# Seven products in place of eight for the last two value blocks of a 2048-wide input projection

## Chip, cores and metric

One NeuronCore of a Trainium2 chip runs one program that computes two transformer blocks over 256 tokens of width 2048. The metric is the device time in microseconds of that program, the median of its runs. The times are in us throughout.

## The reference, cut to what matters

The first block starts with gated linear attention. Its input projection gives queries and keys (1024 columns each), values and output gates (2048 each) and 16 columns of a low-rank gate.

```python
def _gla_mixer(h, w_in, w_gate_up, b_gate, o_norm, w_out):
    proj = h @ w_in
    q, k, v, r, g_low = jnp.split(proj, [...], axis=-1)
    log_a = jax.nn.log_sigmoid(g_low @ w_gate_up + b_gate) / 16
    # chunks of 64 tokens, 4 heads: state = decay * state + k^T v, o = q state
    ...
    return (rmsnorm(o) * o_norm * jax.nn.silu(r)) @ w_out

h = h + _gla_mixer(_rmsnorm(h, gla_norm), ...)
h = h + _sq_relu_mlp(_rmsnorm(h, mlp_norm), ...)
# second block: a hybrid of three attentions, cross-attention to a memory, a gated FFN
```

Here `h @ w_in` is 256 x 2048 times 2048 x 6160, in float32. What the change touches are 1024 of its columns: value columns 1024 to 2047.

## The kernel before

**Numbers.** All large products run in three parts. A float32 weight w is split into a high part (`w_hi`, rounded to the matmul's 32-bit format) and a low part (`w_lo`, the rest), the activations likewise, and TensorE adds high x high, high x low and low x high. So each piece of weights costs ScalarE one rounding copy (line 1226, `split` of ScalarE) and VectorE one subtraction (line 1912, `split` of VectorE), both 128x2048.

**Chunks.** The weights of the whole program are one stream of 1 MB pieces, 128 partitions x 4 x 512: four blocks of 128 input rows (a quarter `q` of the 2048) times 512 output columns (a block `b`). TensorE's `chunk` (lines 632 to 648) multiplies one piece with both halves of the tokens (m = 0, 1): 4 x 2 x 3 = 24 matmuls of 128x128 by 128x512, into the accumulator `acc[:, b % 2]`. Four chunks in turn finish a block. The input projection is items 0 to 47: blocks 0, 1 queries, 2, 3 keys, 4 to 7 values, 8 to 11 output gates.

**The ring.** `SLOTS = 4` pieces are resident in `w_raw` (the low part is written in place, `w_lo`) and in `w_hi`. SyncE loads piece n when item n - 4 is used (line 533). All engines walk the same list of steps, each in its own program order: at step c ScalarE and VectorE split item c + 3 (`AHEAD = 3`), ScalarE when item c - 1 is used, VectorE when the high part is there. TensorE takes item c when its low part is ready. So an item's low part is made while the three before it are multiplied.

**Side work by steps.** The order is written out by hand. After each finished block ScalarE evacuates the accumulator with the row scale (line 1243): to `nat` for queries and keys, to `v` for values. VectorE turns `nat` to the transposed layout in 32x32 tiles (`block_turned`, line 2065): at steps 8, 10 the queries, at steps 20, 24 the keys, each as 8 + 8 transposes with the split of that step between. At step 26 it multiplies the keys with their decay (line 2096), at step 27 the queries of head 0 (`scaled_q`, line 2004). TensorE computes the scores of head hd at step 33 + 4 hd and the products with the values at step 34 + 4 hd (`gla_scores`, `gla_values`). The decays are computed on the way; `la_diff` reaches 2 when the last of them is formed (line 2092).

**Pairs of blocks in seven products.** Elsewhere the kernel already computes two neighbouring blocks with fewer multiplications: for the upper half of the input rows (q = 0, 1) and two column blocks the 2 x 2 x 2 half-size products are replaced by seven (Strassen's scheme in Winograd's form), each of 12 matmuls (`product`); the lower half (q = 2, 3) stays as four chunks. This costs additions: sums of token halves (`s_raw`, with high and low parts `s_hi`, `s_lo`, lines 2118 to 2127) and sums of weight pieces (`T1` to `T4`, lines 2140 to 2150), which enter the list of items as additional ones without a load of their own. In the first MLP pair (`up_pair`, items 8 to 18 of a group of 38, from about 424 us) and in the six like it in the MLP this stands already, and in two pairs of the last FFN: nine in all (`PAIRS`). In the MLP the four sums of rows are lines 2121 to 2124, the second and third sums of weights lines 2143 and 2145.

Of the kernel before, what the change touches and what calls it, by code (L numbers as in the profile page):

```python
# [2 lines left out]
P = 128  # L3
# [14 lines left out]
def build(nc, x, x_turned, mem, mem_turned, stream, cols, rows, wglow, wab, wgu, shapes, masks, out):  # L18
# [23 lines left out]
    PAIRS = GROUPS + 5  # L42
# [5 lines left out]
    with ExitStack() as ctx:  # L48
# [99 lines left out]
        for t in ("f1", "f2", "f3", "f4", "f22"):  # L148
            sum_raw[t] = sb(f"raw_{t}", [P, CH], F32, a_sum[t])
            sum_lo[t] = sb(f"lo_{t}", [P, CH], F32R, a_sum[t])  # L150
# [131 lines left out]
        down_out = sem("down_out")  # L282
        OUT = {name: k for k, name in enumerate(("p1", "p6", "p7", "up2", "up3", "s"))}
# [150 lines left out]
        C_GLA, C_OUT, C_MLP, C_2 = 0, 48, 64, 64 + sum(LENGTH)  # L434
# [12 lines left out]

        def sum_of(i):

            if i >= C_FFN:  # L450
# [11 lines left out]

        def up_chunk(g, q, b):
            return C_MLP + 32 * g + 4 * b + q

        def down_chunk(g, q, b):
            return C_MLP + 32 * g + 16 + 4 * b + q
# [4 lines left out]
        def source(i):  # L472

            if i < C_MLP:
                return i
# [10 lines left out]
            return C_MLP + 32 * g + (k if k < 8 else k - 3)  # L486
# [10 lines left out]
        def summed(i):  # L497

            n = pair_of(i)
            return 4 * n + SUMS[2 if n >= 7 else n % 2].index(sum_of(i)) + 1  # L500
# [5 lines left out]
        def _(sp):  # L506
# [115 lines left out]
        def _(pe):  # L622
# [114 lines left out]
            def gla_values(hd):  # L737
                g = tps.name[("o", hd)]
                open_group(g)
                tps.wait(pe, tps.name[("s", hd)])  # L740
# [12 lines left out]

            pe.wait_ge(junk_set, 1)
            for _ in range(13):
                pe.matmul(acc[:, 1, 0, :], junk[:, 0:P], junk[:], start=True, stop=True)
            for c in range(48):
                b, q = divmod(c, 4)
                chunk(C_GLA + c, X, 4 * q, accs.name[("gla", b)], q == 0, q == 3)
# [18 lines left out]

            def product(c, xh, xl, dst, start=False, stop=False):

                pe.wait_ge(lo_ready, ready(c))
                wh = w_hi[:, c % SLOTS].rearrange("p (k n) -> p k n", n=N)
                wl = low_part(c).rearrange("p (k n) -> p k n", n=N)
                for k in range(4):
                    pe.matmul(dst, xh[:, k], wh[:, k], start=start and k == 0, stop=False, skip_group_check=not start)  # L785
                    pe.matmul(dst, xh[:, k], wl[:, k], start=False, stop=False, skip_group_check=not start)  # L786
                    mm = pe.matmul(dst, xl[:, k], wh[:, k], start=False, stop=stop and k == 3, skip_group_check=not start)  # L787
                mm.then_inc(used, 1)

            def up_pair(g):  # L790
# [17 lines left out]
                if g == 0:  # L808
                    pe.wait_ge(s_formed, 2)
# [46 lines left out]
            for g in range(GROUPS):  # L856
# [11 lines left out]
                if g < 3:  # L868
                    pe.wait_ge(pair_out, pair_step(g, "p7"))
                    down_pair(C_MLP + GROUP * g, accs.name["down", g, 2], accs.name["down", g, 3], (u_hi, u_lo), 2 * g + 4, 5 * g)  # L870
# [315 lines left out]
            for g in range(2):  # L1186
                for c in range(48):
# [3 lines left out]
                    if c == 40:  # L1191
                        down_pair(F_PART[g] + 13, accs.name["fdown", g, 2], accs.name["fdown", g, 3], (uf_hi, uf_lo), 10 + 2 * g, 15 + 5 * g, g == 1)
                        break
# [12 lines left out]
        def _(act):  # L1206
# [8 lines left out]
            def split(c):  # L1215

                if c < NITEM:
                    if sum_of(c) in ("b22", "d22", "f22"):
# [76 lines left out]
            def gla_side(c):  # L1295
# [8 lines left out]
                for hd in range(4):  # L1304
# [13 lines left out]
                    if c == 35 + 4 * hd:  # L1318

                        act.wait_ge(used, c + 1)  # L1320
# [25 lines left out]
            for c in range(64):  # L1346
# [6 lines left out]
                for n in {7: (0, 1), 11: (2,), 15: (3,), 19: (4,), 23: (5,), 27: (6,), 31: (7,)}.get(c, ()):  # L1353
# [49 lines left out]
                if c:  # L1403
                    split(c + AHEAD)
# [41 lines left out]
            for part in range(4):  # L1446
                for c in range(LENGTH[part]):
# [26 lines left out]
                    if part == 0 and c == 6:  # L1474
                        act.wait_ge(s_formed, 1)
                        act.activation(s_hi[:].rearrange("p s k t -> p (s k t)"), s_raw[:].rearrange("p s k t -> p (s k t)"), ACT.Copy).then_inc(pair_out, 1)
                    if part < 3 and c == 23:
                        act.wait_ge(s_formed, 2 * part + 3)
# [356 lines left out]
            for part in range(2):  # L1835
                for c in range(51):
# [22 lines left out]
                    if c == 37:  # L1859
                        act.wait_ge(s_formed, 9 + 2 * part)  # L1860
# [38 lines left out]
        def _(dve):  # L1899
# [169 lines left out]
            for c in range(64):  # L2069
# [23 lines left out]
                if c == 26:  # L2093
# [5 lines left out]
                if c == 27:  # L2099
                    dve.wait_ge(kd_exp, 2)  # L2100
                    scaled_q(0)
                gla_side(c)
                if c - 48 in (6, 7, 11, 15):
                    n = (6, 7, 11, 15).index(c - 48)
                    add_to_h(("glaout", n), n, last=c)
# [5 lines left out]
                if c and c not in (8, 10, 20, 24):  # L2111
                    split(c + AHEAD)
# [871 lines left out]
```

## Time and profile before

| | us |
|---|---|
| median of 3 runs | 2467.79 (2467.27 to 2468.34) |
| the profiled execution | 2466.79 |
| its span, first to last instruction | 2464.6 |
| busy: TensorE / VectorE / ScalarE / GpSimd | 2453.2 / 1710.7 / 1624.5 / 33.4 |
| mean granted TensorE clock | 0.999 of full speed |

How to read the rows below. PE is TensorE's matmuls, PEld its loads of weights, DVE VectorE, ACT ScalarE, POOL GpSimd, SP SyncE, which issues most transfers. A row names the line of the kernel, the operation, the tile written and those read. In a timeline row the first number is the start, the second the time from there to the end of the last of the merged instructions; the bracket holds idle time ahead of it and what ended it. A matmul's duration (0.39) is longer than the distance to the next, since matmuls are pipelined; the distance is the cost.

### The profile page before, as it was taken

The numbers are of one execution on the slowest core, as the hardware profiler recorded it, in microseconds if no ns is written. First come the engines' busy times: TensorE is split into PE (matmuls) and PEld (weight loads), VectorE is DVE, ScalarE is ACT, GpSimd is POOL, SyncE is SP. The second block draws the span as 40 slices with busy tenths as digits, with TensorE's granted clock in tenths as the row PEclk, the third lists the DMA queues.
The fourth block names the chain that finished last, engine by engine and source line by source line (L and its number), as shares of the span: only waits on it lengthen the run. The fifth ranks groups of instructions, "written<-read, shape, count | busy, mean of one in ns | idle before, by whom it ended". The sixth has DMA issues, their size and how long they took to land.

```text
span 2464.6 us, 29831 instructions
## 1 busy us (share of the span) xinstructions
PE 2453.2 (100%) x12343; PEld 2026.5 (82%) x12343; DVE 1710.7 (69%) x1412; ACT 1624.5 (66%) x2127; POOL 33.4 (1%) x41
## 2 busy tenths in 40 slices
PE   9999999999999999999999999999999999999998
PEld 7887788888888888888888888888888888888887
DVE  5775658787778868577765685545666667776678
ACT  6645778856748658776465684535587688748874
POOL 0000000000000000000000000000000000000000
PEclk9999999999999999999999999999999999999999
DMA  8554456545554555545443455555654555645563
GB/s 290 188 191 168 174 188 239 188 182 210 206 204 174 219 208 188 188 172 193 159 148 140 155 185 188 194 199 188 263 198 172 188 190 198 227 171 188 193 233 120
DMA packets 69366, 472.36 MB, mean 192 GB/s; under 512 B 7912, under 2 KB 8352, under 8 KB 13424
## 3 DMA queue, kind: packets, MB, share of 16 engines
q1 hardware_dynamic: 67040, 460.62, 51.5%
q0 software_dynamic: 1312, 7.73, 0.8%
q8 instruction: 97, 1.59, 0.3%
q10 hardware_dynamic: 880, 2.11, 0.2%
q14 instruction: 37, 0.30, 0.0%
HBM read 468.33 MB, written 2.11 MB: 191 GB/s over the span
## 4 chain that ended last, share of the span: by engine, by line
PE 96%; DVE 2%; ACT 1%; issue 1%; DMA 0%; SPq 0%; POOLq 0%; POOL 0%; DVEq 0%; ACTq 0%
PE acc L643 29%; PE acc L644 28%; PE acc L645 28%; PE tp L787 1%; PE tp L785 1%; PE tp L786 1%; PE acc L785 1%; PE acc L787 1%; PE acc L786 1%; DVE w_lo L1912 1%; PE tp L1011 1%; PE tp L944 0%; PE tp L663 0%; DMA w_raw<-in_stream 0%; DVE lo_f L1912 0%
## 5 line engine op out<-in xcount | busy, mean ns | idle before, releaser
L1912 DVE TENSOR_TENSOR w_lo<-w_raw,w_hi 128x2048 fp32r<-128x2048 f32 x412 | 941.2, 2287 | 574.4 <-ACT w_hi L1226 572.6
L1226 ACT ACTIVATE w_hi<-w_raw 128x2048 fp32r<-128x2048 f32 x412 | 788.0, 1915 | 363.4 <-DMA w_raw<-in_stream 303.6
L643 PE MATMUL acc<-w_hi,x_hi 128*128 128x512 f32 (+1 forms) x2112 | 825.3, 391 | 0.7 <-issue 0.3
L644 PE MATMUL acc<-w_lo,x_hi 128*128 128x512 f32 (+1 forms) x2112 | 818.6, 388 | 0.0
L645 PE MATMUL acc<-w_hi,x_lo 128*128 128x512 f32 (+1 forms) x2112 | 818.6, 388 | 0.0
L643 PEld LDWEIGHTS acc<-w_hi,x_hi 128*128 128x128 f32 x2112 | 396.7, 188 | 85.5 <-issue 2.5
L645 PEld LDWEIGHTS acc<-w_hi,x_lo 128*128 128x128 f32 x2112 | 396.6, 188 | 82.0
L644 PEld LDWEIGHTS acc<-w_lo,x_hi 128*128 128x128 f32 x2112 | 396.9, 188 | 80.0 <-issue 1.0
L643 PE MATMUL acc<-w_hi,a_hi 128*128 128x512 f32 x960 | 374.2, 390 | 0.1
L645 PE MATMUL acc<-w_hi,a_lo 128*128 128x512 f32 x960 | 373.5, 389 | 0.0
L644 PE MATMUL acc<-w_lo,a_hi 128*128 128x512 f32 x960 | 373.5, 389 | 0.0
L643 PEld LDWEIGHTS acc<-w_hi,a_hi 128*128 128x128 f32 x960 | 180.2, 188 | 38.2 <-DVE a_lo L2693 0.5
L645 PEld LDWEIGHTS acc<-w_hi,a_lo 128*128 128x128 f32 x960 | 180.2, 188 | 37.5
L644 PEld LDWEIGHTS acc<-w_lo,a_hi 128*128 128x128 f32 x960 | 180.2, 188 | 37.0
L1419 ACT ACTIVATE sq<-turned 32x256 f32<-32x256 f32 x256 | 106.3, 415 | 6.8 <-DVE turned L2247 3.4
L1816 ACT ACTIVATE fm<-fturned 32x256 f32<-32x256 f32 x256 | 106.2, 415 | 4.4 <-DVE fturned L2799 1.4
L1243 ACT ACTIVATE nat<-acc,rstd 128x512 f32<-128x512 f32 (+1 forms) x80 | 50.0, 677 | 73.9 <-PE acc L645 72.5
L1243 ACT ACTIVATE nat<-acc,rhalf 128x512 f32<-128x512 f32 x36 | 22.8, 685 | 66.1 <-PE acc L645 66.1
L1988 DVE TENSOR_TENSOR h<-acc,h 128x1024 f32<-128x1024 f32 x34 | 41.4, 1219 | 18.6 <-PE acc L645 18.6
L1265 ACT ACTIVATE sq<-turned 32x256 f32<-32x256 f32 x112 | 46.5, 415 | 10.2 <-DVE turned L1955 8.9
L643 PE MATMUL acc<-w_hi,m_hi 128*128 128x512 f32 x128 | 49.8, 389 | 0.0
L644 PE MATMUL acc<-w_lo,m_hi 128*128 128x512 f32 x128 | 49.8, 389 | 0.0
(523 smaller groups left out, 2139.4 us busy)
## 6 DMA issues: line engine op xcount, KB each, us to landing
w_raw<-in_stream SPq DMA_DIRECT2D x412, 1024.0 KB, 4.8
w_raw<-in_stream SPq DMA_DIRECT2D x16, 256.0 KB, 7.8
raw_T<-in_stream SPq DMA_DIRECT2D x4, 1024.0 KB, 7.5
raw_b<-in_stream SPq DMA_DIRECT2D x4, 1024.0 KB, 9.2
raw_f<-in_stream SPq DMA_DIRECT2D x4, 1024.0 KB, 8.0
raw_t<-in_stream SPq DMA_DIRECT2D x3, 1024.0 KB, 7.0
raw_d<-in_stream SPq DMA_DIRECT2D x3, 1024.0 KB, 10.2
h<-in_x SPq DMA_DIRECT2D x4, 512.0 KB, 14.7
```

Source lines behind the costliest of these rows:

```text
L643: pe.matmul(dst, xh, wh[:, k], start=first and k == 0, stop=False)
L644: pe.matmul(dst, xh, wl[:, k], start=False, stop=False)
L645: mm = pe.matmul(dst, xl, wh[:, k], start=False, stop=last and k == n_k - 1)
L785: pe.matmul(dst, xh[:, k], wh[:, k], start=start and k == 0, stop=False, skip_group_check=not start)
L786: pe.matmul(dst, xh[:, k], wl[:, k], start=False, stop=False, skip_group_check=not start)
L787: mm = pe.matmul(dst, xl[:, k], wh[:, k], start=False, stop=stop and k == 3, skip_group_check=not start)
L1226: act.activation(w_hi[:, c % SLOTS], raw(c), ACT.Copy).then_inc(hi_ready, 1)
L1243: ins = act.activation(dst[:, m], src[:, m], func, scale=scales[:, j, m:m + 1])
L1265: ins = act.activation(dst[32 * to:32 * to + 32, :, :, q], src[32 * q:32 * q + 32, :, :, to], ACT.Copy, scale=scale)
L1419: ins = act.activation(dst[32 * to:32 * to + 32, :, :, q], src[32 * q:32 * q + 32, :, :, to], ACT.Square)
L1816: ins = act.activation(dst[32 * to:32 * to + 32, :, :, q], src[32 * q:32 * q + 32, :, :, to], ACT.Copy)
L1912: dve.tensor_tensor(low_part(c), raw(c), w_hi[:, c % SLOTS].bitcast(F32), ALU.subtract).then_inc(lo_ready, 1)
```

## The change

Value blocks 2 and 3 of the projection (accumulator blocks 6 and 7, items 24 to 31) are computed in the scheme of seven products. The list of items grows by three there: items 24 to 34 are the pair (`V_PAIR = 16`, its k runs from 8 to 18), the output gates move from items 32 to 47 to items 35 to 50, everything behind by three. On each engine:

- SyncE issues, behind the load of item 22, two more loads for pieces (q 0, b 3) and (q 1, b 3) of the value columns into `g3` and `g22`, after `la_diff` is 2. Their pieces are no longer loaded by the ring, so the bytes stay equal.
- VectorE forms sums of x at step 3 and of its rows at step 19, their low part at step 22, the sums of weights g1, g3, g2, g4 at steps 21, 22, 23, 26, and adds the partial results to `v` at steps 33, 34, 35. It splits three more items. The scaling of the keys moves from step 26 to 28, that of head 0's queries from 27 to 31. The turning of the keys at steps 20 and 24 is as before.
- ScalarE rounds the sums of rows at step 21, copies the shared partial result out of PSUM at steps 26, 30 and 32 (four copies), scales the values at steps 33 and 36 where it evacuated them at steps 27 and 31, and splits three more items.
- TensorE runs `v_pair` for items 24 to 34.

```diff
-        for n in range(8):
+        for n in range(6):
             accs.add(("gla", n), "act")
-        for n in range(8, 12):
+        for n in range(6, 12):
             accs.add(("gla", n), "dve")
...
+        V_SUM_AT = {10: "g22", 12: "g1", 13: "g2", 15: "g3", 16: "g4"}
...
+                if c == V_PAIR + 6:
+                    sp.wait_ge(la_diff, 2)
+                    sp.dma_start(sum_raw["g3"][:], stream[v_chunk(0, 3)]).then_inc(v_b_in, 16)
+                    sp.dma_start(sum_raw["g22"][:], stream[v_chunk(1, 3)]).then_inc(v_b_in, 16)
...
+            def v_pair():
...
+                tps.wait(pe, tps.name["z1"])
+                product(c0 + 8, *of_x(0, 0), chain, start=True, stop=True)
+                chunk(c0 + 9, X, 8, left, True, False)
+                pe.wait_ge(s_formed, 2)
+                accs.wait(pe, right - 2)
+                product(c0 + 10, *of_s(3), acc[:, right % 2, 0], start=True)
+                chunk(c0 + 11, X, 12, left, False, True)
+                product(c0 + 12, *of_s(0), both, start=True, stop=True)
+                pe.wait_ge(v_taken, 2)
+                product(c0 + 13, *of_s(1), chain, stop=True)
+                product(c0 + 14, *of_x(1, 0), acc[:, left % 2, 0], stop=True)
+                pe.wait_ge(v_taken, 3)
+                product(c0 + 15, *of_s(2), chain, stop=True)
+                product(c0 + 16, *of_x(1, 1), acc[:, left % 2, 1], stop=True)
+                chunk(c0 + 17, X, 8, right, False, False, rows_=(0,), done=False)
+                chunk(c0 + 17, X, 8, right, True, False, rows_=(1,))
+                chunk(c0 + 18, X, 12, right, False, True)
...
+            def v_sums(i):
...
+                if i == 19:
+                    dve.tensor_tensor(s_raw[:, 2], rows_[0][0], rows_[1][0], ALU.subtract)
+                    link(dve.tensor_tensor(s_raw[:, 0], rows_[1][0], rows_[1][1], ALU.subtract))
+                    link(dve.tensor_tensor(s_raw[:, 1], s_raw[:, 0], rows_[0][0], ALU.subtract))
+                    dve.tensor_tensor(s_raw[:, 3], s_raw[:, 1], rows_[0][1], ALU.add).then_inc(s_formed, 1)
+                if i == 22:
+                    dve.wait_ge(v_taken, 1)
+                    dve.tensor_tensor(s_lo[:], s_raw[:], s_hi[:].bitcast(F32), ALU.subtract).then_inc(s_formed, 1)
+            def v_pair(k):
...
+                if k == 5:
+                    b11 = weights_in(8)
+                    dve.wait_ge(v_b_in, 32)
+                    dve.tensor_tensor(sum_raw["g1"][:], b11, sum_raw["g3"][:], ALU.add).then_inc(v_sum_ready, 1)
+                if k == 6:
...
+                    dve.tensor_tensor(sum_raw["g3"][:], sum_raw["g3"][:], sum_raw["g22"][:], ALU.add).then_inc(v_sum_ready, 1)
+                if k == 7:
+                    dve.tensor_tensor(sum_raw["g2"][:], sum_raw["g1"][:], sum_raw["g22"][:], ALU.add).then_inc(v_sum_ready, 1)
+                if k == 10:
+                    b21 = weights_in(14)
+                    dve.wait_ge(used, V_PAIR + 11)
...
+                    dve.tensor_tensor(sum_raw["g4"][:], sum_raw["g2"][:], b21, ALU.add).then_inc(v_sum_ready, 1)
...
+            for i in range(67):
+                c = i if i < 32 else i - 3 if i >= 35 else -1
+                v_pair(i - V_PAIR)
...
-                if c == 26:
+                if c == 28:
                     dve.wait_ge(kd_exp, 1)
                     dve.wait_ge(q_turned, 4)
                     link(dve.tensor_tensor(kT[:], kT[:], kd[:], ALU.mult))
...
-                if c == 27:
+                if c == 31:
                     dve.wait_ge(kd_exp, 2)
+                    dve.wait_ge(used, V_PAIR + 14)
                     scaled_q(0)
...
-                if c and c not in (8, 10, 20, 24):
-                    split(c + AHEAD)
+                if i and i not in (8, 10, 20, 24):
+                    split(i + AHEAD)
+                v_sums(i)
```

## Rows read from the trace of the kernel before

**Rows 1.** The page, its parts 1 (busy us, share) and 4 (chain).

```profile
PE 2453.2 (100%) x12343; PEld 2026.5 (82%) x12343; DVE 1710.7 (69%) x1412; ACT 1624.5 (66%) x2127; POOL 33.4 (1%) x41
...
PE 96%; DVE 2%; ACT 1%; issue 1%; DMA 0%; SPq 0%; POOLq 0%; POOL 0%; DVEq 0%; ACTq 0%
```

**Rows 2.** TensorE's waits over the span: total, times, longest; first and last of seven.

```profile
PE acc L756 <- DVE junk L2042: 1.2, 1, 1.2
...
PE tp L892 <- DVE cqT L2333: 0.2, 1, 0.2
```

**Rows 3.** TensorE's timeline, 100 us on: first and 57th matmul without a gap.

```profile
99.76 0.39 PE L644 MATMUL acc<-w_lo,x_hi 128*128 128x512 f32 x1
...
112.45 0.39 PE L643 MATMUL acc<-w_hi,x_hi 128*128 128x512 f32 x1
```

**Rows 4.** ScalarE's timeline, 56 to 146 us: evacuations (L1243) and a high part.

```profile
56.01 1.27 ACT L1243 ACTIVATE nat<-acc,rstd 128x512 f32<-128x512 f32 x2 [1.12 <-PE acc L645]
...
122.85 1.26 ACT L1243 ACTIVATE v<-acc,rstd 128x512 f32<-128x512 f32 x2 [4.07 <-PE acc L645]
124.01 1.91 ACT L1226 ACTIVATE w_hi<-w_raw 128x2048 fp32r<-128x2048 f32 x1
...
144.61 1.26 ACT L1243 ACTIVATE v<-acc,rstd 128x512 f32<-128x512 f32 x2 [4.22 <-PE acc L645]
```

**Rows 5.** Busy time of the engines in two stretches: length; PE, PEld, DVE, ACT, POOL.

```profile
125.95:168.65 42.70, 42.70 (x190) 35.35 (x189) 35.63 (x46) 16.86 (x12) 0.00 (x0) 1.00 0.54 190
398.00:455.00 57.00, 57.00 (x252) 46.95 (x251) 51.55 (x33) 45.15 (x55) 0.71 (x1) 1.00 0.50 182
```

**Rows 6.** VectorE's timeline, 43 to 167 us: low parts (L1912), key turning, key scaling.

```profile
43.72 2.29 DVE L1912 TENSOR_TENSOR w_lo<-w_raw,w_hi 128x2048 fp32r<-128x2048 f32 x1 [0.22 <-ACT w_hi L1226]
...
116.52 0.17 DVE L2092 TENSOR_TENSOR edec<-edec,cum 128x8 f32<-128x8 f32 x1
...
125.95 2.29 DVE L1912 TENSOR_TENSOR w_lo<-w_raw,w_hi 128x2048 fp32r<-128x2048 f32 x1 [4.85 <-ACT w_hi L1226]
128.16 3.57 DVE L2065 STREAM_TRANSPOSE kT<-nat 32x256 f32<-32x256 f32 x8
131.75 2.29 DVE L1912 TENSOR_TENSOR w_lo<-w_raw,w_hi 128x2048 fp32r<-128x2048 f32 x1
134.07 3.60 DVE L2065 STREAM_TRANSPOSE kT<-nat 32x256 f32<-32x256 f32 x8
137.69 2.29 DVE L1912 TENSOR_TENSOR w_lo<-w_raw,w_hi 128x2048 fp32r<-128x2048 f32 x1
...
161.66 2.28 DVE L2096 TENSOR_TENSOR kT<-kT,kd 128x2048 f32<-128x2048 f32 x1
...
164.37 2.29 DVE L1912 TENSOR_TENSOR w_lo<-w_raw,w_hi 128x2048 fp32r<-128x2048 f32 x1
```

**Rows 7.** VectorE's timeline in the first MLP pair: the operations that the change adds.

```profile
401.67 2.35 DVE L2118 TENSOR_TENSOR x_sum<-x_hi,x_lo 128x1024 f32<-128x1024 f32 x2
...
407.40 0.68 DVE L2121 TENSOR_TENSOR s_raw<-x_sum 128x512 f32<-128x512 f32 x1
...
409.44 0.69 DVE L2124 TENSOR_TENSOR s_raw<-s_raw,x_sum 128x512 f32<-128x512 f32 x1
...
421.44 2.28 DVE L2145 TENSOR_TENSOR raw_T<-raw_T,raw_b 128x2048 f32<-128x2048 f32 x1
423.65 2.28 DVE L1912 TENSOR_TENSOR w_lo<-w_raw,w_hi 128x2048 fp32r<-128x2048 f32 x1
```

**Rows 8.** Transfers issued from 325 to 465 us: count, size, median us to landing.

```profile
w_raw<-in_stream SPq DMA_DIRECT2D x25, 1024.0 KB, 4.9
raw_T<-in_stream SPq DMA_DIRECT2D x1, 1024.0 KB, 6.9
raw_b<-in_stream SPq DMA_DIRECT2D x1, 1024.0 KB, 8.9
```

**Rows 9.** TensorE's timeline at the start: the 13 matmuls on a zeroed tile.

```profile
1.19 5.73 PE L756 MATMUL acc<-junk 128*128 128x512 bf16 x13 [1.19 <-DVE junk L2042]
```

More of the change, by code:

```diff
@@ L41, in build @@
     LENGTH = [38, 38, 38, 35]
-    PAIRS = GROUPS + 5
+    PAIRS = GROUPS + 6
     NITEM = stream.shape[0] + 3 * PAIRS
@@ L432, in build @@
             add_quarter(6, n)
-        C_GLA, C_OUT, C_MLP, C_2 = 0, 48, 64, 64 + sum(LENGTH)
+        C_GLA, C_OUT, C_MLP, C_2 = 0, 51, 67, 67 + sum(LENGTH)
+        V_PAIR = 16
         C_BR, C_WO, C_X, C_XO, C_FFN = C_2 + 50, C_2 + 114, C_2 + 130, C_2 + 142, C_2 + 146
@@ L739, in gla_values @@
                 open_group(g)
+                if hd == 0:
+                    accs.wait(pe, accs.name["gla", 7])
                 tps.wait(pe, tps.name[("s", hd)])
@@ L751, in gla_side, with product, of_x, of_s @@
                         gla_values(hd)
+            def product(c, xh, xl, dst, start=False, stop=False):
+                pe.wait_ge(lo_ready, ready(c))
+                wh = w_hi[:, c % SLOTS].rearrange("p (k n) -> p k n", n=N)
+                wl = low_part(c).rearrange("p (k n) -> p k n", n=N)
+                for k in range(4):
+                    pe.matmul(dst, xh[:, k], wh[:, k], start=start and k == 0, stop=False, skip_group_check=not start)
+                    pe.matmul(dst, xh[:, k], wl[:, k], start=False, stop=False, skip_group_check=not start)
+                    mm = pe.matmul(dst, xl[:, k], wh[:, k], start=False, stop=stop and k == 3, skip_group_check=not start)
+                mm.then_inc(used, 1)
+            def v_pair():
+                c0, left, right = V_PAIR, accs.name["gla", 6], accs.name["gla", 7]
+                chain, both = tpf(0)[:, 0:N], tpf(0)[:, N:2 * N]
+                def of_x(q, m):
+                    return [t[:, 4 * q:4 * q + 4, m * P:(m + 1) * P] for t in X]
+                def of_s(n):
+                    return s_hi[:, n], s_lo[:, n]
+                tps.wait(pe, tps.name["z1"])
[15 more added lines that the diff above has]
+                chunk(c0 + 18, X, 12, right, False, True)
             pe.wait_ge(junk_set, 1)
@@ L757, in _ @@
             for c in range(48):
+                if c == 24:
+                    v_pair()
+                if 24 <= c < 32:
+                    continue
                 b, q = divmod(c, 4)
-                chunk(C_GLA + c, X, 4 * q, accs.name[("gla", b)], q == 0, q == 3)
+                chunk(C_GLA + (c if c < 24 else c + 3), X, 4 * q, accs.name[("gla", b)], q == 0, q == 3)
                 if c == 3:
@@ L777, in _ @@
                 gla_side(48 + c)
[L779 to L788, printed above, removed]
             def up_pair(g):
@@ L1345, in _ @@
             act.activation(wg[:, :, 0:16], wg_raw[:], ACT.Copy).then_inc(wg_h, 1)
-            for c in range(64):
+            def v_pair(k):
+                left, right = [slice(n * N, (n + 1) * N) for n in (2, 3)]
+                chain = tpf(0)[:, 0:N]
+                if k == 5:
+                    act.wait_ge(s_formed, 1)
+                    act.activation(s_hi[:].rearrange("p s k t -> p (s k t)"), s_raw[:].rearrange("p s k t -> p (s k t)"), ACT.Copy).then_inc(v_taken, 1)
+                if k == 10:
+                    act.wait_ge(used, V_PAIR + 9)
+                    act.activation(v[:, 0, left], chain, ACT.Copy).then_inc(v_taken, 1)
+                if k == 14:
+                    act.wait_ge(used, V_PAIR + 14)
+                    act.activation(v[:, 0, right], chain, ACT.Copy, scale=-1.0).then_inc(v_taken, 1)
+                if k == 16:
+                    act.wait_ge(used, V_PAIR + 16)
+                    act.activation(v[:, 1, left], chain, ACT.Copy)
+                    act.activation(v[:, 1, right], chain, ACT.Copy, scale=-1.0).then_inc(v_taken, 1)
+                if k == 17:
+                    accs.wait(act, accs.name["gla", 6])
+                    row_scaled(0, v[:, :, left], v[:, :, left])
+                if k == 20:
+                    accs.wait(act, accs.name["gla", 7])
+                    row_scaled(0, v[:, :, right], v[:, :, right])
+            for i in range(67):
+                c = i if i < 32 else i - 3 if i >= 35 else -1
+                v_pair(i - V_PAIR)
                 if c == 4:
@@ L2067, in block_turned @@
                     ins.then_inc(q_turned, 1)
-            for c in range(64):
+            def v_sums(i):
+                rows_ = [[x_sum[:, q, :, m * P:(m + 1) * P] for q in range(2)] for m in range(M)]
+                if i == 3:
+                    for q in range(2):
+                        ins = dve.tensor_tensor(x_sum[:, q], x_hi[:, 4 * q:4 * q + 4].bitcast(F32), x_lo[:, 4 * q:4 * q + 4].bitcast(F32), ALU.add)
+                    link(ins)
+                if i == 19:
[6 more added lines that the diff above has]
+                    dve.tensor_tensor(s_lo[:], s_raw[:], s_hi[:].bitcast(F32), ALU.subtract).then_inc(s_formed, 1)
@@ L2070, in _ @@
+            for i in range(67):
+                c = i if i < 32 else i - 3 if i >= 35 else -1
+                v_pair(i - V_PAIR)
                 if c == 6:
@@ L2104, in _ @@
                     n = (6, 7, 11, 15).index(c - 48)
-                    add_to_h(("glaout", n), n, last=c)
+                    add_to_h(("glaout", n), n, last=i)
                     norm_turned(1, n, ("glaout", n))
```

68 lines of the change are left out of this document (53 added, 15 removed).

## The prediction

> **What bounds the kernel now.** I read the page first, then TensorE's waits, then the two engines that feed it. TensorE is busy for the whole span and nearly the whole chain that ended last is TensorE's [rows 1]. Its longest wait is 1.2 us at the very start; the view names seven kinds, from this one down to 0.2 us, and they come to 3.3 us in all [rows 2]. So the time is the number of matmuls times their cadence, as long as VectorE delivers every low part in time. The cadence of the 128x512 matmuls is (112.45 - 99.76) / 56 = 0.2266 us [rows 3]. A chunk is 24 of them, 5.44 us; ScalarE's evacuations of value blocks 0 and 1 (from chunks 19 and 23) come 144.61 - 122.85 = 21.76 us apart, four chunks [rows 4], the same number. A half chunk (one `product`, 12 matmuls) is 2.72 us.
>
> The second view to read is VectorE in the stretch that changes. From 125.95 to 168.65 us it is busy 35.6 of 42.7 us [rows 5]; its idle time lies ahead of low parts and ends with ScalarE's high part [rows 6]. That is not a bound today, but it is little room.
>
> **What is removed.** The old loop spends 8 chunks, 192 matmuls, on value blocks 2 and 3. The new `v_pair` has seven products of 12 and four chunks of 24: 84 + 96 = 180. Twelve matmuls go: 12 x 0.2266 = 2.72 us of pure TensorE time. That is the whole possible gain, 0.11% of 2467.79. About 0.2% (4.9 us) is what a measurement of this kernel can tell from no change. With nothing late, the result would be 2465.1.
>
> **What is added.** In place of 8 items (24 to 31) there are 11 (24 to 34). Each item is one upper part on ScalarE (1.91 us) and one low part on VectorE (2.29 us, 2.20 to 2.21 from start to start when they follow on) [rows 4, 6, 7]. So three more of each. VectorE also gets: the two sums of x at step 3 (2.35 us [rows 7]); four formings of sums of rows at step 19 (four 128x512 additions, 407.40 to 410.13, 2.73 us [rows 7]); their low part at step 22; four sums of weights (g1, g3, g2, g4) of one 128x2048 addition each at steps 21 to 26; three 128x1024 additions at steps 33 to 35. What VectorE already does there stays: the turning of the keys in four runs of eight transposes at steps 20 and 24, 3.59 and 3.62 us a run, and the scaling of the keys [rows 6]. The scaling of keys goes from step 26 to 28 and that of queries from 27 to 31. Both still stand ahead of a low part in VectorE's order. In the diff the turning of the keys itself isn't touched.
>
> **The sum, on VectorE.** VectorE works in order, so I add what lies between two fixed points. The first is the start of the low part of item 22 at 125.95: it waits for the upper part that ScalarE makes from 124.01 on, right after its evacuation at 122.85, which itself waits for chunk 19 [rows 4, 6]. Nothing of the change moves that, and work cannot slide ahead of it. The second is the low part of item 31. Between them, in program order (g1, g3, s_lo, g2, g4 are the additions of 128x2048):
> - low parts 22 to 31: 10 x 2.21 = 22.1, and 0.1 more for each of the two that a run of transposes follows (131.75 to 134.07 is 2.32 [rows 6]): 22.3
> - the four formings: 2.7
> - the four runs of transposes: 2 x 3.59 + 2 x 3.62 = 14.4
> - g1, g3, g2, g4 and s_lo: 5 x 2.20 = 11.0 (the same operations took this in the first MLP pair [rows 7])
> - scaling of the keys and two memsets, 161.66 to 164.37 [rows 6]: 2.7
>
> Together 53.1 us: low part 31 is finished at 125.95 + 53.1 + 0.1 = 179.15. When does TensorE want it? Chunk 23's result is there at 144.61 [rows 4]. Items 24 to 30 hold nine half chunks (1, 2, 1, 2, 1, 1, 1): 9 x 2.72 = 24.5, so item 31 is due to begin at 169.1 on that scale. A first matmul starts some 0.2 us ahead of the preceding result and has its load of weights, 0.19 us, before it, so the low part is wanted about 0.4 earlier, at 168.7. It comes 179.15 - 168.7 = 10.45 us late. Walking item by item with the same durations spreads it: item 24 waits 0.7, 25 1.7, 26 1.2, 27 3.1 (the whole first run of key transposes stands ahead of it), 28 0.5, 29 1.7, 31 1.7, together 10.6. The same walk over the old order, begun at 51 us, puts low part 29 at 164.34 where the trace has it at 164.37 [rows 6], which is why I trust it.
>
> From item 32 on the low parts catch up: item 32 has 0.5 us of slack, 33 has 1.0, 34 has 3.2, 35 has 5.3, since items 33 and 34 are full chunks and no more sums stand between. Net: 10.5 - 2.7 = **+7.8 us**.
>
> **What costs nothing, and its cover.** ScalarE: the rounding of the sums (1.9), three more upper parts and four copies out of PSUM. It is busy 16.9 of 42.7 us in the stretch [rows 5] and its upper parts are ready before VectorE comes to each. TensorE's waits for the copies: the copy after item 29 is needed after item 30, 2.7 us later, and takes half of an evacuation, 0.64 [rows 4]. SyncE: the two added transfers wait for `la_diff` to be 2, which is true from 116.7 on [rows 6], while SyncE gets there at about 117.4; so this wait blocks nothing. The loads queued behind are the question. Load 23 issues at 122.9, when chunk 19 is done, and a load by itself takes 4.9 us to land [rows 8]. With 2 MB ahead of it in the queue, issued at about 118, it lands later; the same kind of pair took 6.9 and 8.9 us to land [rows 8], so the second is in at about 127 and load 23 some 2.5 us behind it, at about 130 instead of 127.8. Its upper part is then done at about 131.6, and VectorE reaches low part 23 only at 134.5. Cost 0; if the landing were 5 us later still, about 2 us, which I put into the upper end. The sums of x at step 3 lie ahead of low part 7. That one starts at 43.72 and takes 2.29 [rows 6]; item 7 is the last of its block, whose result is there at 56.01 [rows 4], so it is wanted at 56.01 - 5.44 - 0.4 = 50.2. The 4.2 us in hand cover the 2.35. The last additions and ScalarE's scaling of the values end near 203.5 in the walk, the values are first read after 212, and the block that follows needs its accumulator released at item 35, with 5 us to spare.
>
> Bounds of what no row shows: the sums' extra waits (0 each if they pass, 0.05 us for each of about 8 instructions as upper end), the pipeline delay at a stalled start (0.2 to 0.6 us instead of 0.4, once in the net), and VectorE's rate beside other work (the first MLP pair shows 2.2 for the same operations with ScalarE busy 45 of 57 us [rows 5, 7]). These make the net +7.3 to +8.6, and +10.5 with the late landing. Against that, if some of VectorE's operations overlap better than in any row, 3 us less: +4.5.
>
> **The rivals.** (A) Forecast: VectorE's backlog outweighs the matmuls saved: 2467.79 + 7.8 = **2475.6**; against the profiled execution (2466.79, span 2464.6) that is 2474.6 and a span of 2472.4. (B) The lead of three items absorbs it. Low part 22 is done at 128.2 and wanted at 133.3, so there are 5 us in hand before anything starts; in the first MLP pair VectorE is busy 51.6 of 57 us [rows 5] with sums and splits of the same sizes, and the list of TensorE's waits has none from there. It decides from the point where the sum above is 42.7 or less; it would take 10.4 us of VectorE's 53.1 to be gone or to fit before 125.95. Against it: in the first MLP pair no key turning (14.4) and scaling (2.7) stand between. Then 2465.1, the same within 0.2%. (C) The added transfers delay the ring so that ScalarE becomes late first: up to 2478. (D) TensorE's clock falls in the gaps. Today the granted clock is 1.00 in the stretches read [rows 5] and 0.999 over the span (table above), and the only slow matmuls are the 13 at the start, 5.73 / 13 = 0.44 us each, the level of 1.2 GHz [rows 9]. The longest new gap is 3.1 us, ahead of item 27. At half clock each half chunk in items 27 to 30 takes 5.4 instead of 2.7; while VectorE is the bound this is hidden in part (the five half chunks would take 13.6 more, of which the waits of 28, 29 and 31, 3.9 us, can absorb a share), so 5 to 10 us more: 2481 to 2486.
>
> The Trainium skill, page "TensorE: Matmul & The Clock Gate", Part 1, says that the array's clock is gated to half when TensorE has been idle long enough, which is the rule behind (D). This case's trace shows a granted clock of 1.00 throughout but has no gap of this kind after the start, so it neither confirms nor denies it; by the page the change could lose more than the waits, and without it the sum stands as above.
>
> **How the numbers follow.** (A) 0.78, (B) 0.10, (C) 0.05, (D) 0.05, and 0.02 for something in this first stage turning out faster than before. The range takes (A) with its bounds and (C): 2472.3 (net +4.5) to 2479.5; outside it stay (B), (D) and the rest. Slower by over 0.2% (above 2472.7): 0.86. Within 0.2%: 0.12. Faster by over 0.2%: 0.02.
>
> **What would show it.** In the profile after: TensorE's waits for another engine grow from about 3 us to about 14, nearly all on low parts (L1912's successor), between 144 and 180 us, at `product` and `chunk` alike, the largest ahead of item 27; VectorE without a gap from 126 to 179, ScalarE's upper parts ready before it; behind the pair the evacuations arrive about 7.8 us later than before (item 35 begins near 196 instead of 188) and this shift stays constant to the end. The forecast is wrong if TensorE shows no waits there (then B), if VectorE has gaps ended by ScalarE or a DMA (then C), or if the granted clock is under 1.00 after a gap (then D).

## The result and the profile after

| | before | after |
|---|---|---|
| median, us | 2467.79 (7 runs, 2467.21 to 2468.68) | 2475.06 (7 runs, 2474.01 to 2475.59) |
| ratio after / before | | 1.003, 95% interval 1.0021 to 1.0039 |
| profiled execution, its span | 2466.79, 2464.6 | 2475.24, 2473.4 |
| TensorE matmuls | 12343 | 12331 |
| busy TensorE / VectorE / ScalarE | 2453.2 / 1710.7 / 1624.5 | 2453.6 / 1736.3 / 1633.4 |

The changed kernel does its 12 matmuls less and is 7.3 us slower; 7.8 was forecast. The first view to open is again TensorE's waits, of the changed kernel between 100 and 200 us (who waited for whom; total, times, longest us):

```profile
PE acc L664 <- DVE w_lo L1999: 4.0, 2, 2.7
PE tp L783 <- DVE lo_g L1999: 2.0, 2, 1.4
PE acc L783 <- DVE lo_g L1999: 1.0, 1, 1.0
PE tp L783 <- DVE w_lo L1999: 0.4, 1, 0.4
```

The kernel before has no row in this stretch. All of these wait for a low part (L1999 is the subtraction that was L1912), at items 24 to 31, and for nothing else. L664 is in `chunk`, L783 in `product`. TensorE's timeline puts them in order, the bracket being the idle time:

```profile
145.84 0.47 PE L783 MATMUL tp<-w_hi,x_hi 128*128 128x512 f32 x1 [0.42 <-DVE w_lo L1999]
150.15 0.50 PE L664 MATMUL acc<-w_hi,x_hi 128*128 128x512 f32 x1 [1.31 <-DVE w_lo L1999]
156.85 0.47 PE L783 MATMUL acc<-w_hi,s_hi 128*128 128x512 f32 x1 [0.97 <-DVE lo_g L1999]
162.56 0.80 PE L664 MATMUL acc<-w_hi,x_hi 128*128 128x512 f32 x1 [2.70 <-DVE w_lo L1999]
173.00 0.47 PE L783 MATMUL tp<-w_hi,s_hi 128*128 128x512 f32 x1 [0.61 <-DVE lo_g L1999]
180.12 0.47 PE L783 MATMUL tp<-w_hi,s_hi 128*128 128x512 f32 x1 [1.39 <-DVE lo_g L1999]
```

These are items 24, 25, 26, 27, 29 and 31. The brackets sum to 7.4 us, less than what is lost: a matmul counts as busy for 0.39 us where the next could start after 0.23, which hides 0.16 of every wait; the second matmul behind a wait comes 0.31 to 0.34 us after the first instead of 0.23; and the clock, below, adds 1.5 us at item 27. The full loss is read from the ends. VectorE's timeline of the same kernel, with what the kernel before has as [rows 6]:

```profile
126.81 2.29 DVE L1999 TENSOR_TENSOR w_lo<-w_raw,w_hi 128x2048 fp32r<-128x2048 f32 x1 [4.85 <-ACT w_hi L1287]
129.02 0.68 DVE L2164 TENSOR_TENSOR s_raw<-x_sum 128x512 f32<-128x512 f32 x1
...
131.68 3.57 DVE L2152 STREAM_TRANSPOSE kT<-nat 32x256 f32<-32x256 f32 x8
135.26 2.29 DVE L1999 TENSOR_TENSOR w_lo<-w_raw,w_hi 128x2048 fp32r<-128x2048 f32 x1
137.58 3.59 DVE L2152 STREAM_TRANSPOSE kT<-nat 32x256 f32<-32x256 f32 x8
141.20 2.29 DVE L2183 TENSOR_TENSOR raw_g<-w_raw,raw_g 128x2048 f32<-128x2048 f32 x1
143.41 2.29 DVE L1999 TENSOR_TENSOR w_lo<-w_raw,w_hi 128x2048 fp32r<-128x2048 f32 x1
...
177.68 4.49 DVE L1999 TENSOR_TENSOR lo_g<-raw_g,w_hi 128x2048 fp32r<-128x2048 f32 x2
```

From 126.81 on no row has a bracket until 194: VectorE never waits there, and TensorE waits for nothing but its low parts. The low part of item 24 starts at 143.41, where the kernel before had it at 137.69. Low part 31 (the first of the two in the last row) ends at 177.68 + 2.29 = 179.97, and item 31's first matmul starts at 180.12, 0.15 later.

Everything in this execution is some 0.86 us later than in the profile before already at the first evacuations (ScalarE's second block at 56.87 for 56.01 [rows 4]), from two waits of 0.18 and 0.65 us for low parts of the very first pieces, at 6.3 and 10.2 us. That has nothing to do with the change: the first operation that the change adds starts at 44.30, and the experiments below on the kernel before have the same evacuation at 56.30 to 56.63. With 0.86 added, low part 31 was forecast for 180.0. ScalarE's evacuation behind chunk 23 is here at 145.46. Item 31 was due 24.5 us after the start of item 24's first matmul at 145.46 - 0.2, so at 169.8: it is 10.4 us late; 10.45 was forecast. The first addition to `h` starts at 330.80 before and at 339.43 after: 8.63 later, less 0.86 is 7.8.

The granted clock, as the stretches of TensorE show it (last three columns: clock, DMA share, GB/s):

```profile
155.00:160.00 5.00, 3.89 (x16) 2.56 (x15) 4.90 (x9) 1.96 (x2) 0.00 (x0) 1.00 0.58 205
160.00:165.00 5.00, 2.44 (x6) 1.96 (x7) 4.89 (x8) 1.86 (x1) 0.00 (x0) 0.71 0.02 8
165.00:170.00 5.00, 5.00 (x23) 4.10 (x22) 4.94 (x5) 0.24 (x1) 0.00 (x0) 0.95 0.00 0
```

After the wait of 2.70 us the clock had fallen: the first seven matmuls of item 27 (162.56 to 165.62) take 3.1 us instead of 1.6, 0.43 us apart, the lower level of 1.2 GHz; then 0.23 again. That is rival (D)'s mechanism, and by the prediction's own list ("if the granted clock is under 1.00 after a gap") the sign of (D). Its price is settled below.

### The profile page after: what moved, and what is told of

The parts are those of the page before. It is cut to its first block, busy times and chain, and to the rows that moved or that the text cites. A ratio compares the mean times of both kernels' runs of the same rounds, so it can differ in the third digit from the quotient of the medians.

```text
span 2473.4 us, 29846 instructions
## 1 busy us (share of the span) xinstructions
PE 2453.6 (99%) x12331; PEld 2024.5 (82%) x12331; DVE 1736.3 (70%) x1429; ACT 1633.4 (66%) x2135; POOL 33.5 (1%) x41
## 4 chain that ended last, share of the span: by engine, by line
PE 92%; DVE 4%; ACT 1%; issue 1%; DMA 1%; SPq 0%; POOLq 0%; POOL 0%; DVEq 0%; ACTq 0%
PE acc L664 27%; PE acc L665 27%; PE acc L666 27%; DVE w_lo L1999 1%; PE tp L783 1%; PE tp L785 1%; PE tp L784 1%; PE acc L783 1%; PE acc L785 1%; PE acc L784 1%; DMA w_raw<-in_stream 1%; ACT w_hi L1287 1%; DVE kT L2152 1%; PE tp L1068 1%; PE tp L1001 0%
## 5 line engine op out<-in xcount | busy, mean ns | idle before, releaser
L1999 DVE TENSOR_TENSOR w_lo<-w_raw,w_hi 128x2048 fp32r<-128x2048 f32 x410 | 936.5, 2287 | 554.3 <-ACT w_hi L1287 552.5
L664 PE MATMUL acc<-w_hi,x_hi 128*128 128x512 f32 (+1 forms) x2080 | 813.8, 391 | 5.7 <-DVE w_lo L1999 4.6
L666 PE MATMUL acc<-w_hi,x_lo 128*128 128x512 f32 (+1 forms) x2080 | 806.7, 388 | 0.0
L665 PE MATMUL acc<-w_lo,x_hi 128*128 128x512 f32 (+1 forms) x2080 | 806.6, 388 | 0.0
L664 PEld LDWEIGHTS acc<-w_hi,x_hi 128*128 128x128 f32 x2080 | 391.0, 188 | 91.1 <-DVE w_lo L1999 7.2
L666 PEld LDWEIGHTS acc<-w_hi,x_lo 128*128 128x128 f32 x2080 | 390.9, 188 | 80.5
L665 PEld LDWEIGHTS acc<-w_lo,x_hi 128*128 128x128 f32 x2080 | 391.1, 188 | 79.1 <-issue 1.0
L664 PE MATMUL acc<-w_hi,a_hi 128*128 128x512 f32 x960 | 374.1, 390 | 0.1
L664 PEld LDWEIGHTS acc<-w_hi,a_hi 128*128 128x128 f32 x960 | 180.2, 188 | 38.1 <-DVE a_lo L2835 0.5
L664 PE MATMUL acc<-w_hi,m_hi 128*128 128x512 f32 x128 | 49.8, 389 | 0.0
## 6 DMA issues: line engine op xcount, KB each, us to landing
raw_b<-in_stream SPq DMA_DIRECT2D x4, 1024.0 KB, 10.2
```

Of the source, the lines that this page charges most:

```text
L664: pe.matmul(dst, xh, wh[:, k], start=first and k == 0, stop=False)
L665: pe.matmul(dst, xh, wl[:, k], start=False, stop=False)
L666: mm = pe.matmul(dst, xl, wh[:, k], start=False, stop=last and k == n_k - 1)
L1999: dve.tensor_tensor(low_part(c), raw(c), w_hi[:, c % SLOTS].bitcast(F32), ALU.subtract).then_inc(lo_ready, 1)
```

## The experiments

Theory V is the forecast's: the work that VectorE does in order between low part 22 and low part 31 is longer than TensorE can wait. Rival T blames the added transfers and the ring, rival P the products themselves. Each kernel was timed beside the kernel before on the same chip; "against" is that one's median beside it. "By the trace" means the start of the first addition to `h` (330.80 us in the kernel before), less what the execution was already late at the first evacuations; by it the changed kernel is 7.8 us late.

### Key turning taken apart

```diff
-                if c in (8, 10, 20, 24):
+                if c in (8, 10):
...
+                for n, quadrants in {11: ((2, (0, 1)),), 12: ((2, (2,)),), 13: ((2, (3,)),), 17: ((3, (0,)),), 19: ((3, (1,)),), 20: ((3, (2,)),), 27: ((3, (3,)),)}.get(c, ()):
+                    accs.wait(dve, accs.name[("gla", n)])
+                    block_turned(n, quadrants)
...
-                if c == 28:
+                if c == 30:
                     dve.wait_ge(kd_exp, 1)
...
-                if i and i not in (8, 10, 20, 24):
+                if i and i not in (8, 10):
```

> The changed kernel with the turning of the keys taken apart: block 2's four quadrants at steps 11, 11, 12, 13, block 3's at steps 17, 19, 20, 27, and the scaling of the keys at step 30 instead of 28. Same operations, other places. Theory V (VectorE's in-order work from low part 22 to 31 sets TensorE's waits): five of the eight quadrants leave that stretch and fill idle time, 12.6 us of VectorE's 53 stay ahead no longer; my walk with the trace's durations gives no wait for a low part at all, so 2467.8 - 2.7 = 2465.1, and TensorE's waits in the stretch 0 to 0.5 us. Rival T (the added transfers and the ring make the items late): the waits stay near 8 to 10 us, 2473 to 2475. Rival P (the products cost by themselves, by waits for the partial results in PSUM or by restarts): 2469 or more.

Measured: 2464.89 us against 2467.22, ratio 0.9991 (0.9982 to 1.0). It was timed once more:

> The same kernel as the one with the key turning taken apart, once more beside the kernel before, for its interval: 2.7 us below it by V, 2464.6 to 2465.1.

2464.70 against 2467.34, ratio 0.9989 (0.998 to 0.9998). In the first one's profile TensorE has no wait between 100 and 215 us, with VectorE still almost always busy (its stretches; PE, PEld, DVE, ACT):

```profile
125.00:144.00 19.00, 19.00 (x86) 15.73 (x85) 18.72 (x18) 9.38 (x6) 0.00 (x0) 1.00 0.71 273
144.00:180.00 36.00, 36.00 (x161) 29.81 (x160) 35.07 (x25) 22.05 (x16) 0.00 (x0) 1.00 0.40 147
```

161 matmuls in the 36 us from 144 on. The changed kernel, in the same stretch:

```profile
144.00:180.00 36.00, 28.72 (x115) 21.76 (x113) 35.62 (x32) 18.40 (x13) 0.00 (x0) 0.95 0.35 120
```

Products, transfers, sums and TensorE's program are the same in both. So neither T nor P: with VectorE's work placed otherwise the 12 matmuls come back as 2.3 and 2.6 us, where 2.7 was worked out. This version is the fastest of the three, by 0.1% against the kernel before, which the second series of runs just tells from nothing (the first one's interval ends at 1.0).

VectorE's timeline shows where a piece went, here one quadrant of step 19 (x4, where a run was x8):

```profile
122.66 2.29 DVE L1999 TENSOR_TENSOR w_lo<-w_raw,w_hi 128x2048 fp32r<-128x2048 f32 x1 [2.12 <-ACT w_hi L1287]
124.99 1.78 DVE L2152 STREAM_TRANSPOSE kT<-nat 32x256 f32<-32x256 f32 x4
126.85 2.29 DVE L1999 TENSOR_TENSOR w_lo<-w_raw,w_hi 128x2048 fp32r<-128x2048 f32 x1
...
165.01 4.49 DVE L1999 TENSOR_TENSOR lo_g<-raw_g,w_hi 128x2048 fp32r<-128x2048 f32 x2
```

Before low part 22 there were 4.85 us of idle time; here a quadrant fills a part of them, and low part 22 still starts as soon as its high part is there. From its start to the end of low part 31 (165.01 + 2.29) it is 40.5 us, where the changed kernel needs 53.2: six of the eight quadrants (the expectation says five) and the scaling of the keys now stand outside. Low part 31 is done at 167.3. By the prediction's reckoning it is wanted at 169.6, ScalarE's evacuation behind chunk 23 being at 145.51 here, so TensorE doesn't wait.

The walk missed one thing. TensorE has one new wait, ahead of item 14, where two quadrants at step 11 now stand in front of the low part:

```profile
90.78 0.50 PE L664 MATMUL acc<-w_hi,x_hi 128*128 128x512 f32 x1 [0.30 <-DVE w_lo L1999]
```

By the trace this kernel is 2.1 us ahead of the kernel before in both series, so the placing itself costs about 0.6 of the 2.7.

### Only block 2's turning moved

```diff
-                if c in (8, 10, 20, 24):
+                if c in (8, 10, 24):
...
+                for n, quadrants in {11: ((2, (0, 1)),), 12: ((2, (2,)),), 13: ((2, (3,)),)}.get(c, ()):
...
```

> The changed kernel with only block 2's key turning moved (steps 11, 11, 12, 13 instead of 20), block 3's left at step 24. V: by the walk waits of 0.8, 0.5, 1.7 and 1.7 us ahead of items 27, 28, 29 and 31, none ahead of 24 to 26, together 4.6 instead of 10.5: 2467.8 + 4.6 - 2.7 = 2469.7. It is less than 7.2 us of transposes saved, since part of them would come to stand as idle time of VectorE. T or P: 2473 to 2475, with the waits ahead of 24 to 26 still there.

Measured: 2469.47 against 2467.22, ratio 1.0009 (1.0 to 1.0018). The waits, on TensorE's timeline, are those of the walk, one by one, once 0.2 to 0.3 us is added to each bracket (forecast 0.8, 0.5, 1.7, 1.7):

```profile
156.93 0.50 PE L664 MATMUL acc<-w_hi,x_hi 128*128 128x512 f32 x1 [0.41 <-DVE w_lo L1999]
162.87 0.50 PE L783 MATMUL tp<-w_hi,s_hi 128*128 128x512 f32 x1 [0.17 <-DVE lo_g L1999]
167.37 0.47 PE L783 MATMUL tp<-w_hi,s_hi 128*128 128x512 f32 x1 [1.46 <-DVE lo_g L1999]
174.48 0.47 PE L783 MATMUL tp<-w_hi,s_hi 128*128 128x512 f32 x1 [1.39 <-DVE lo_g L1999]
```

None stands ahead of items 24 to 26 any more; the small one ahead of item 14 is here too.

### The four formings two steps earlier

```diff
-                if i == 19:
+                if i == 17:
                     dve.tensor_tensor(s_raw[:, 2], rows_[0][0], rows_[1][0], ALU.subtract)
```

> The changed kernel with the four formings of the sums of rows (2.7 us of VectorE) at step 17 instead of 19, so ahead of the idle time before low part 22. V: low parts 24 and on come 2.7 us earlier; waits 0.9, 3.1, 0.5, 1.7, 1.7 ahead of items 26, 27, 28, 29, 31, together 7.9: 2472.3 to 2473. T or P: no change, 2475.1.

Measured: 2472.67 against 2467.22, ratio 1.0021 (1.0012 to 1.003). 2.7 us of VectorE's work went ahead of the fixed point, and by the medians 2.4 to 2.6 us of time with it (2475.1 or 2475.3 to 2472.7). The waits ahead of items 24 and 25 are gone. By the trace the gain is 2.0, and VectorE's and ScalarE's timelines say where the other 0.7 went:

```profile
131.18 1.92 ACT L1287 ACTIVATE w_hi<-w_raw 128x2048 fp32r<-128x2048 f32 x1 [4.57 <-DMA w_raw<-in_stream]
133.13 2.29 DVE L1999 TENSOR_TENSOR w_lo<-w_raw,w_hi 128x2048 fp32r<-128x2048 f32 x1 [0.70 <-ACT w_hi L1287]
```

What stands ahead of low part 22 is free and what stands behind it is paid for; that fixed point is shown. But with 2.7 us less in front of it VectorE now reaches low part 23 before its high part, whose load lands late behind the two added transfers, and waits 0.70 us. So rival T has a small share here, as the next limit behind VectorE's work.

### Block 3's turning in one run at step 26

```diff
-                if c in (8, 10, 20, 24):
+                if c in (8, 10, 20):
...
+                for n, quadrants in {26: ((3, (0, 1, 2, 3)),)}.get(c, ()):
...
```

> The changed kernel with block 3's key turning as one run of sixteen transposes (four quadrants, 7.2 us) at step 26 instead of eight before and eight behind the low part of step 24. The sum of VectorE's work up to low part 31 is the same. V in its strong form (only the sum counts, a gap elsewhere is given back): the wait of 3.1 us ahead of item 27 vanishes, a wait of about 5.2 us ahead of item 29 appears, the sum stays 10.4, and the time stays 2475 within 0.5. If instead each gap counts by itself (by the clock that falls in a long one), the time goes up by 1 to 3 us; if shorter gaps at items 27 were a loss of their own, it goes down by 1 to 3.

Measured: 2475.29 against 2467.22, ratio 1.0032 (1.002 to 1.0044), so 8.1 us over the kernel before where the change has 7.3. The wait moved as expected (its timeline):

```profile
155.93 0.47 PE L783 MATMUL acc<-w_hi,s_hi 128*128 128x512 f32 x1 [0.96 <-DVE lo_g L1999]
171.95 0.76 PE L783 MATMUL tp<-w_hi,s_hi 128*128 128x512 f32 x1 [4.86 <-DVE lo_g L1999]
172.51 0.63 PE L784 MATMUL tp<-lo_g,s_hi 128*128 128x512 f32 x1
...
177.63 0.55 PE L784 MATMUL acc<-w_lo,x_hi 128*128 128x512 f32 x1
```

Behind the longer wait 14 matmuls run slower, the last of them at 177.63, and item 31 has no wait of its own left: the lower clock took it. The intervals don't tell 8.1 from 7.3. By the trace this kernel is 8.8 us late where the changed one is 7.8: the 14 matmuls from 171.95 to 178.03 took 6.1 us where 3.2 are due, 2.9 more, and the wait that item 31 would have had hid about 1.9 of it. "Only the sum counts" holds but for what the lower clock adds, about a microsecond here.

### The kernel before with the turning in the other places

The edit is that of the first experiment, made to the kernel before, where the scaling goes from step 26 to 30.

> The kernel before with the key turning and scaling placed as in the experiment that takes them apart (steps 11, 11, 12, 13, 17, 19, 20, 27; scaling at step 30). V: TensorE waits for no low part there today, so nothing is to be gained: 2467.8, the same within 0.5. If the placing had a merit of its own, it would show here as 1 us or more.

Measured: 2467.74 against 2467.29, ratio 1.0002 (0.9992 to 1.0011). The placing is worth nothing by itself; it pays only where VectorE is late. The trace even has it 0.6 us behind, with the same wait of 0.29 us ahead of item 14 as its one new wait.

### The kernel before with idle additions on VectorE

```diff
+                for _ in range({21: 1, 22: 2, 23: 1, 26: 1}.get(c, 0)):
+                    link(dve.tensor_tensor(idle[:], x_hi[:, 0:8].rearrange("p k t -> p (k t)").bitcast(F32), x_hi[:, 0:8].rearrange("p k t -> p (k t)").bitcast(F32), ALU.add))
```

> The kernel before with five idle additions of 128x2048 on VectorE (2.3 us each, 11.5 in all) at steps 21, 22, 22, 23 and 26, where the change puts its sums of weights and low part; nothing else of the change. V with the lead of three items: the full chunks leave room, the walk gives one wait of about 0.8 to 1.2 us ahead of item 29, so 2468.5 to 2469. If VectorE's work were paid for in full, 2479; if there were room for all, 2467.8.

Measured: 2468.31 against 2467.29, ratio 1.0004 (0.9995 to 1.0013), one wait, 0.95 us, at the expected place. The second with twice the counts:

> The same with ten idle additions (23.1 us) at steps 21 to 26. V: now beyond the room; the walk gives waits of 0.4, 6.0, 1.4, 0.4, 0.5, 4.1 us ahead of items 24 to 29, together 12.7: 2480.5. So the second five cost about 12 us where the first five cost 1. A rival that puts the loss on the products or transfers has VectorE's load cost little: under 2472.

Measured: 2481.23 against 2467.29, ratio 1.0055 (1.0038 to 1.0072). Its trace has not the six waits of the walk but two, ahead of items 25 and 29, each with the lower clock behind it, which swallows the small ones between:

```profile
156.60 0.80 PE L644 MATMUL acc<-w_hi,x_hi 128*128 128x512 f32 x1 [5.75 <-DVE w_lo L1913]
184.76 0.79 PE L644 MATMUL acc<-w_hi,x_hi 128*128 128x512 f32 x1 [3.83 <-DVE w_lo L1913]
```

Five additions cost 1.0 us, ten 13.9: the lead of three items is a store that is used up first. Beyond it the second five, 11.6 us of VectorE's work, cost 12.9: one for one, and about a microsecond more, which the lower clock behind the last wait can account for. No product and no added transfer is in these kernels, so VectorE's load alone makes the loss.

### The added transfers alone

```diff
+                if c == 22:
+                    sp.wait_ge(la_diff, 2)
+                    for n in range(2):
+                        sp.dma_start(idle[n][:], stream[28 + n]).then_inc(idle_in, 16)
...
                 if c == 27:
+                    dve.wait_ge(idle_in, 32)
```

> The kernel before with the two added transfers alone: 2 MB behind the load of item 22, after the same wait, into space that nothing reads. V: load 23 lands about 2 us later, ScalarE's upper part 23 ends about 2 us later, no wait of TensorE: 2467.8 within 0.5. T: part of the loss shows here, 2470 or more.

Measured: 2466.20 against 2467.29, ratio 0.9996 (0.9986 to 1.0005). The later landing is there on ScalarE's timeline and harms nobody:

```profile
124.30 1.91 ACT L1232 ACTIVATE w_hi<-w_raw 128x2048 fp32r<-128x2048 f32 x1
130.33 1.92 ACT L1232 ACTIVATE w_hi<-w_raw 128x2048 fp32r<-128x2048 f32 x1 [4.12 <-DMA w_raw<-in_stream]
```

High part 23 starts at 130.33 instead of 127.66, and TensorE waits for nothing in the stretch. So T is out as the cause of the loss; what is left of it are the 0.7 us that showed when the formings went forward. That the median is 1 us lower has no cause that I know; the interval includes no change, and by the trace this kernel is level with the kernel before.

### What the lower clock costs where nothing hides it

The kernel before with five, then seven idle additions at step 30 (`{30: 5}`, `{30: 7}` in the diff above).

> The kernel before with five idle additions (11.6 us) on VectorE at step 30, ahead of low part 33, in a stretch where VectorE has room and catches up at once. One wait, no backlog behind it. The walk gives 1.5 us ahead of item 33 and none behind: 2467.3 to 2467.8 plus 1.5 = 2469.0. TensorE's granted clock stays at 1.00, as after the waits of up to 1.4 us in the changed kernel.

Measured: 2468.73 against 2467.34, ratio 1.0006 (0.9997 to 1.0015); one wait of 1.24 us, the clock at 1.00 behind it.

> The same with seven (16.2 us). The walk gives one wait of 6.1 us ahead of item 33: 2473.6 by the wait alone. After waits of 2.7, 3.8, 4.9 and 5.8 us in the runs so far the granted clock had fallen and 6 to 12 matmuls came at 0.43 instead of 0.23 us apart. Where VectorE was still behind, that was hidden. Here nothing behind the wait is late, so it should show: 1.2 to 2.5 us more, 2475 to 2476. If the lower clock costs nothing, 2473.6.

Measured: 2474.67 against 2467.34, ratio 1.0031 (1.0019 to 1.0044). Its timeline of TensorE:

```profile
199.80 0.79 PE L644 MATMUL acc<-w_hi,x_hi 128*128 128x512 f32 x1 [5.84 <-DVE w_lo L1913]
200.39 0.63 PE L645 MATMUL acc<-w_lo,x_hi 128*128 128x512 f32 x1
...
202.52 0.56 PE L644 MATMUL acc<-w_hi,x_hi 128*128 128x512 f32 x1
202.91 0.39 PE L645 MATMUL acc<-w_lo,x_hi 128*128 128x512 f32 x1
```

And the stretches, with the clock third from the right:

```profile
195.00:200.00 5.00, 0.20 (x1) 0.20 (x2) 4.93 (x4) 0.35 (x1) 0.00 (x0) 0.60 0.53 205
200.00:205.00 5.00, 5.00 (x17) 3.98 (x18) 4.14 (x2) 0.00 (x0) 0.00 (x0) 0.71 0.00 0
```

The two added additions are 4.6 us of VectorE and cost 2474.67 - 2468.73 = 5.9 by the medians: 1.3 us are left for the clock. The intervals are wider than that, so the traces have to carry it, and they do: the one with seven is 6.0 us behind the one with five, 1.4 more than 4.6, and its seven matmuls from 199.80 to the one at 202.91 take 3.1 us for 1.6. Even where nothing hides it, it is 1 to 2 us.

## Why the prediction was right, step by step

- **The gain.** 12343 - 12331 = 12 matmuls, as counted. With the waits gone the kernel is 2.3 and 2.6 us below the one before, for 2.72; by the trace 2.1, since the other placing costs 0.6 itself.
- **The first fixed point.** Low part 22 starts at 126.81, 0.86 behind 125.95, and all is 0.86 late. Moving the formings ahead of it gave 2.0 to 2.6 us of their 2.7 back, the rest being the late high part 23. Shown.
- **The sum.** 126.81 to 179.97 is 53.2; 53.1 + 0.1 was worked out. Every addend was a row of the kernel before. The one term that I had no row for, more waits on the sums, was 0: g1 starts at 141.20 right behind the transposes.
- **The lateness.** 10.4 of 10.45. A stalled first matmul of a product starts 0.15 us behind its low part's end (0.05 in a chunk) where about 0.2 was implied.
- **The waits one by one.** Forecast 0.7, 1.7, 1.2, 3.1, 0.5, 1.7, 1.7. With 0.2 to 0.3 added to each bracket: 0.7, 1.6, 1.2, 3.0, none, 0.9, 1.6. That is 9.0 of the forecast 10.6; the 1.5 us of the lower clock stand in place of the rest. So the sum came out because lateness is set by VectorE's work, whatever TensorE does between; the split into waits was a bit off, and the list of waits over the whole span adds up to 11.7 us for the 14 that were forecast. The difference at items 28 and 29 is the clock: item 27's first matmuls were slow, so TensorE came to item 28 after its low part, and had less to wait at item 29.
- **The cover.** The transfers cost nothing in the changed kernel: high part 23 was done at 132.50, low part 23 started at 135.26. The cover was 2.8 us, and where the formings no longer stood there it was used up. The other high parts of the stretch were early too. The upper end of the range, 2479.5, is 1.2 above what its own sum gives (2467.8 + 10.5 = 2478.3); no reason for it stands there.
- **Rival (B)** was right in kind and short in size: the lead does absorb, as five idle additions (11.5 us for 1.0) show. By the prediction's sum it decides at 42.7 us of work in the stretch, and here there were 53; with the turning placed otherwise there were 40.5, and the wait was gone.
- **Rival (D)** had its mechanism right and its price wrong. I gave the fall of the clock 0.05, and 5 to 10 us, taking it to last over items 27 to 30. It did fall, in the forecast's own case, so (A) and (D) were not the alternatives that they were made out to be. It fell for seven matmuls, 1.5 us, and all of it was hidden since low part 29 was the next thing late. The prediction had foreseen that a part would be hidden while VectorE is the bound, but took the slow time for so long that the waits couldn't hide it. I took a lower clock for a state of the whole stretch, where the only row at hand, the start, already showed how short it is: 13 matmuls [rows 9]. The Trainium skill's page "TensorE: Matmul & The Clock Gate", Part 1, has the rule that an idle array is gated to half its clock and that activity releases it; the traces now agree with both halves: the matmuls came 0.43 us apart behind waits of 2.70 us and more, and 0.23 again 7 to 14 matmuls later.
- **The end.** +7.8 against a measured +7.3, whose own uncertainty is about 2. The profiled pair shows 7.8 once the start's 0.86 is taken off. The last tenths are luck: the terms were good to a few tenths each.

Still open: the series of medians can't tell 7.3 from 7.8, and the order in which the quadrants were placed was chosen from the walk; only this one placing was tried, and it leaves a wait of its own ahead of item 14. One without it, and the formings moved as well, might give the full 2.7.

## What to carry to other kernels

A saving on the engine that bounds a kernel is worth what the engines that feed it can follow. Add up the feeder's work in program order between two fixed points, the last wait that it can't avoid and the low part that is wanted last, and compare with the time in which the bounding engine gets there; a busy share alone (here 35.6 of 42.7 us) doesn't say it. Work with a loose due time that stands in such a stretch is the first to move: the same eight quadrants of transposes, in other places, turned +7.3 us into -2.5.

## What the runs showed of the hardware

- TensorE's granted clock fell to the lower level after waits of 2.70 (in two kernels), 3.83, 4.86, 5.75 and 5.84 us and stayed at 1.00 after waits of up to 1.46. 7 to 14 matmuls of 512 columns then came 0.43 us apart instead of 0.23, and the clock was back. In one of the two with 2.70 (the formings earlier) the clock was still 1.00 over the first three matmuls behind the wait (160.40 to 161.20 us) and 0.55 from there to 165. Where nothing hid it the price was 1.3 to 1.5 us.
- VectorE's additions of 128x2048 in float32 take 2.29 us each but 2.20 from start to start when the next is ready, the same with ScalarE and transfers busy beside them (145.61 to 154.42 us of the changed kernel) as with both nearly idle (166.16 to 170.57). A schedule added up with 2.20 or 2.21, 3.59 to 3.62 for eight transposes and 2.32 for a low part ahead of such a run met a stretch of 53 us within 0.1 us.
